# One network, two blocks: the first feed-forward unrolled, sums and prefetches spread, first tiles halved

## The reference, cut to what matters

```python
def conv_ffn(h, w_up, conv_w, conv_b, w_down, grid):
    gate, up = jnp.split(h @ w_up, 2, axis=-1)              # 1024 -> 2 x 2816
    gate = dwconv_grid(gate, conv_w, conv_b, grid)          # 3x3 depthwise; for the context a row of 256
    return (jax.nn.gelu(gate, approximate=True) * up) @ w_down

def swiglu(u, wg, wu, wd):
    return (jax.nn.silu(u @ wg) * (u @ wu)) @ wd

mod_l = jnp.split((jax.nn.silu(c) @ w_mod[layer] + b_mod[layer])[:, None, :], 6, axis=-1)   # latent
mod_c = jnp.split((jax.nn.silu(c_ctx) @ w_mod[layer] + b_mod[layer])[None, None, :], 6, axis=-1)
hl = modulate(rmsnorm(xl, norm_g[layer, 2]), mod_l[3], mod_l[4])     # h * (1 + scale) + shift
```

## Time and profile before

| | |
|---|---|
| median of 3 runs | 3651.16 us (3646.98 to 3659.4) |
| the profiled execution | 3651.36 us, its span 3649.6 us |
| mean granted clock of PE | 0.92 |
| PE busy | 3164.0 us (87%) |
| DVE busy | 2526.5 us (69%) |
| ACT busy | 1757.7 us (48%) |
| POOL busy | 389.5 us (11%) |
| transfers | 646.02 MB, mean 177 GB/s |

### The profile page before, as it was taken

One profiled execution on the slowest core, in us unless ns is written; L12 is line 12 of the kernel. 1 busy time (PEld: TensorE's weight loads), 2 busy tenths in 40 slices (PEclk: granted clock), 3 DMA queues, 4 the chain that ended last, 5 costly groups with the idle time before them and its releaser, 6 DMA issues. The chain is left out here.

```text
span 3649.6 us, 68684 instructions
## 1 busy us (share of the span) xinstructions
PE 3164.0 (87%) x27312; PEld 2626.4 (72%) x27312; DVE 2526.5 (69%) x3909; ACT 1757.7 (48%) x3042; POOL 389.5 (11%) x355
## 2 busy tenths in 40 slices
PE   5799876999969788877977799878799999999997
PEld 2654445887757477767976699654689889888986
DVE  1436665778874644576876678457599899989986
ACT  1223323112232575534441634336487788778775
POOL 0000002442100121106610011000000000000000
PEclk8899987999979999998978799877799999999998
DMA  8320011325632000036652398320399999999995
GB/s 336 82 83 1 1 46 52 92 92 173 248 98 63 3 5 5 4 123 217 210 194 65 120 365 308 122 72 8 105 371 350 355 362 369 351 356 361 371 347 196
DMA packets 270311, 646.02 MB, mean 177 GB/s; under 512 B 25277, under 2 KB 123689, under 8 KB 269929
## 3 DMA queue, kind: packets, MB, share of 16 engines
q1 hardware_dynamic: 248025, 562.62, 43.3%
q0 software_dynamic: 21312, 77.60, 5.9%
q10 hardware_dynamic: 720, 2.23, 0.2%
HBM read 641.34 MB, written 1.05 MB: 176 GB/s over the span
## 5 line engine op out<-in xcount | busy, mean ns | idle before, releaser
L3992 DVE TENSOR_TENSOR weights_lo<-raw_ring,weights_hi 128x896 fp32r<-128x896 f32 (+1 forms) x376 | 413.4, 1126 | 59.7 <-ACT weights_hi L3952 50.4
L344 PE MATMUL bank_pair<-x_hi,ring_hi 128*128 128x512 f32 (+1 forms) x928 | 349.2, 376 | 87.4 <-DVE x_lo L381 38.0
L3952 ACT ACTIVATE weights_hi<-raw_ring 128x896 fp32r<-128x896 f32 (+1 forms) x376 | 365.4, 981 | 98.0 <-PE bank_pair L3924 98.0
L344 PE MATMUL bank_pair<-x_hi,ring_lo 128*128 128x512 f32 (+1 forms) x928 | 343.7, 370 | 0.0
L3924 PE MATMUL bank_pair<-weights_hi,expert_x_hi 128*128 128x448 f32 x1024 | 296.8, 371 | 5.5 <-DVE weights_lo L3992 5.5
L3924 PE MATMUL bank_pair<-weights_hi,expert_x_lo 128*128 128x448 f32 x1024 | 291.5, 366 | 0.0
L3924 PE MATMUL bank_pair<-weights_lo,expert_x_hi 128*128 128x448 f32 x1024 | 291.5, 366 | 0.0
L3992 DVE TENSOR_TENSOR weights_lo<-H,weights_hi 128x896 fp32r<-128x896 f32 (+1 forms) x240 | 264.2, 1133 | 29.7 <-ACT weights_hi L3952 20.0
L3952 ACT ACTIVATE weights_hi<-H 128x896 fp32r<-128x896 f32 (+1 forms) x240 | 236.7, 989 | 72.7 <-PE bank_pair L3924 72.7
L344 PEld LDWEIGHTS bank_pair<-x_hi,ring_hi 128*128 128x128 f32 x928 | 180.4, 194 | 124.3 <-issue 59.2
L3924 PEld LDWEIGHTS bank_pair<-weights_hi,expert_x_hi 128*128 128x128 f32 x1024 | 190.6, 189 | 22.3 <-issue 5.3
(11 more groups left out here) (745 smaller groups left out, 7705.3 us busy)
## 6 DMA issues: line engine op xcount, KB each, us to landing
raw_ring<-in_moe_w_gate SPq DMA_DIRECT2D x72, 896.0 KB, 6.8
raw_ring<-in_moe_w_up SPq DMA_DIRECT2D x64, 896.0 KB, 7.1
ring_up<-in_ffn_w_up SPq DMA_DIRECT2D x110, 512.0 KB, 3.8
raw_ring<-in_moe_w_down SPq DMA_DIRECT2D x48, 1024.0 KB, 7.4
mod_ring_ada<-in_w_ada POOLq DMA_DIRECT2D x84, 512.0 KB, 6.4
H<-in_moe_w_up SPq DMA_DIRECT2D x48, 896.0 KB, 7.3
ring_down<-in_ffn_w_down SPq DMA_DIRECT2D x66, 512.0 KB, 6.9
H<-in_moe_w_down SPq DMA_DIRECT2D x32, 1024.0 KB, 7.4
```

What stands on the lines that cost most here:

```text
L344: ins = self.core.nc.tensor.matmul(self.banks[o][:, 0:moving.shape[1]], lhs, moving, start=(s == self.first[o] and k == 0 and i == 0), sto ...
L3952: nc.scalar.activation(hi[:, u % CUTS, 0:n].bitcast(F32R), raw_part(u), ACT.Copy).then_inc(cut.sem, 1)
L3992: nc.vector.tensor_tensor(lo[:, u % CUTS, 0:n].bitcast(F32R), raw_part(u)[:, 0:n], hi[:, u % CUTS, 0:n], ALU.subtract).then_inc(parted.sem, 1)
```

## The change

1. `ffn_stage` goes; `ffn_up_stage` serves both layers, unrolled, on `SplitGemm`. With 512 tokens it has three places for cut tiles, ten taps, and the gelu in ACT's order three tiles after the cut that frees the first bank (`gelu_after`), with 256 tokens four (it was two further on). x is cut into parts of Y and H.
2. In both, and in swiglu, the remainders of the first two tiles are DVE's (`rest_by`), tile 0 is cut and made in two halves, one for each output; a tile is cut before the x chunks that go with it, and PE waits for x chunk by chunk. `row_stage` does the first row in two halves.
3. The decoder's sums go in pairs (4, 5), (0, 2), (1, 3). 16 items, those of (4, 5), move into the first up stage, loaded by SP; 32 items (48 operations) stay in the down stage, and DVE's rate there is 2.5 operations a row instead of 2.2 items. Each block of sums is a tensor of its own. The latent stage's sums are loaded behind an iteration's tiles.
4. The prefetches of down weights go out one an iteration: from iteration 3 in the feed-forwards, from tile 8 at every fourth in swiglu.

```diff
@@ ModSums
-        self.items = [(j, k) for a in range(0, n_j, 2) for k in range(DC) for j in (a, a + 1)]
+        self.items = [(j, k) for pair in order for k in range(DC) for j in pair]
+    def ops_of(self, item):
+        return sum(i == item for i, _ in self.ops)
@@ SplitGemm
+    def pieces(self, n):
+        return (slice(0, P), slice(P, 2 * P)) if n == 0 else (slice(0, 2 * P),)
...
+        for cols in self.pieces(n):
+            self.core.nc.scalar.activation(self.hi[n % self.parts][:, 0:kc, cols].bitcast(F32R), self.ring[:, n % self.slots, 0:kc, cols], ACT.Copy).then_inc(self.cut.sem, 1)
...
         for j, o in enumerate(outs):
+            if n == 0 or j == 0:
+                self.wait_rested(pe, n, j if n == 0 else -1)
...
             for k in range(kc):
+                if it == 0 and j == 0:
+                    x.wait(pe, k0 + k)
@@ RowGemm
+    def load_ahead(self, sp):
+        if self.begun < min(self.slots, self.chunks):
+            self.load(sp, self.begun)
+            self.begun += 1
@@ row_stage
+        halves = lambda k: (slice(0, 2), slice(2, 4)) if k == 0 else (slice(0, 4),)
...
-                while waiting and len(sums) - len(waiting) < int((k + 1) * per_row):
+                while waiting and done + waiting[0].ops_of(waiting[0].taken) <= (k + 1) * ops_per_row:
+                    done += waiting[0].ops_of(waiting[0].taken)
                     waiting.pop(0).add(dve)
@@ FfnWeights
-            self.up = column_pairs(core, self.up_ctx, "up", [(up, 0), (up, FF)], FC // 2, ("pool",))
+        self.up = column_pairs(core, self.up_ctx, "up", [(up, 0), (up, FF)], FC // 2, ("dve", "dve", "pool"))
@@ ffn_up_stage
+        own = lambda i: tuple(core.sb(f"up_{n}{i}", [P, 4, 256], ctx=ctx)[:] for n in ("hi", "lo"))
+        g.open([p.const, own(0), own(1)] if T == TT else [p.X_ctx, p.H_ctx, p.Y_ctx, p.const])
+        x = XParts(core, DC, lambda k: st.H[:, k, here], p.Y[:, :, here], lambda k: p.H[:, k, here])
+        gelu_after = 3 if T == TT else 4
...
             for it in range(n_it):
                 for n in range(it * per, (it + 1) * per):
                     g.load_more(sp, n)
+                for _ in range(n_sums * it // n_it, n_sums * (it + 1) // n_it):
+                    sums.load(sp, "sp")
+                if it >= 3:
+                    weights.down.load_ahead(sp)
...
+                g.cut_tile(act, n)
                 for k in range(s * 4, s * 4 + 4) if it == 0 and s < 2 else ():
                     x.cut_chunk(act, k)
+                for due in range(n_it - 1):
+                    if n == due * per + g.parts + 1:
+                        middle_tap(due)
+                    if n == due * per + g.parts + gelu_after:
+                        gelu(due)
...
+            for n in (0, 1):
+                g.rest_of_tile(dve, nc.vector, n)
+                for k in range(4 * n, 4 * n + 4):
+                    x.rest_of_chunk(dve, k)
+            for it in range(n_it):
+                taps(it)
+                for _ in range(n_sums * it // n_it, n_sums * (it + 1) // n_it):
+                    sums.add(dve)
+                products(it)
@@ swiglu_stage
-                        if n == 2 * g.per:
-                            down.start(sp)
+                        if n % g.per == 0 and n >= 2 * g.per:
+                            down.load_ahead(sp)
@@ decoder_sums, build
+    return ModSums(core, st, f"mod{layer}", st.A["w_mod"][layer], ("b_mod", layer * 48), ((0, 48), (1, 16)), ((4, 5), (0, 2), (1, 3)))
+            ffn_up_stage(core, st, weights, 0, TT, sums, 16)
+            sums.sums_in(scope, (0, 1, 2, 3))
             ffn_down_stage(core, st, weights, sums)
```

More of the change, by code:

```diff
@@ L559, with __init__ @@
     WIDE = 1024
-    def __init__(self, core, st, scope, key, w, bias, vecs, slots=4, place=None):
+    def __init__(self, core, st, key, w, bias, vecs, order, slots=4):
         self.core, self.st, self.key, self.slots = core, st, key, slots
@@ L768, in _ @@
                     b = m.blocks.index((v, 2 * q + j // 2))
-                    ins = nc.tensor.matmul(core.bank(i % 4)[32 * j:32 * j + 32], st.C("ones")[:, 0:32], m.sums[:, b, j % 2 * 512:(j % 2 + 1) * 512], start=True, stop=True)
+                    ins = nc.tensor.matmul(core.bank(i % 4)[32 * j:32 * j + 32], st.C("ones")[:, 0:32], m.sums[b][:, j % 2 * 512:(j % 2 + 1) * 512], start=True, stop=True)
                 ins.then_inc(summed.sem, 1)
@@ L1078, in __init__ @@
         self.per = len(tiles)
-        self.rest_by = [rest_by[n % len(rest_by)] for n in range(len(self.tiles))]
+        self.rest_by = [rest_by[min(n, len(rest_by) - 1)] for n in range(len(self.tiles))]
+        assert self.rest_by[0] == "dve"
         self.kc = max(t[2] for t in tiles)
@@ L1167, in settle @@
             c.n += 16 * len(range(i, len(self.tiles), self.slots))
-        for c in (self.cut, self.consumed):
-            c.n += len(self.tiles)
+        self.cut.n += len(self.tiles) + 1
+        self.consumed.n += len(self.tiles)
         for c in self.freed.values():
@@ L1226, in start @@
     def start(self, sp):
-        self.begun = min(self.slots, self.chunks)
-        for k in range(self.begun):
-            self.load(sp, k)
+        while self.begun < min(self.slots, self.chunks):
+            self.load_ahead(sp)
+    def load_ahead(self, sp):
+        if self.begun < min(self.slots, self.chunks):
+            self.load(sp, self.begun)
+            self.begun += 1
     def raw(self, k):
@@ L1291, in _ @@
                     act.wait_ge(consumed.sem, consumed.at(k - S + 1))
-                nc.scalar.activation(places[k % S][0].bitcast(F32R), g.raw(k), ACT.Copy).then_inc(cut.sem, 1)
+                for q in halves(k):
+                    nc.scalar.activation(places[k % S][0][:, q].bitcast(F32R), g.raw(k)[:, q], ACT.Copy).then_inc(cut.sem, 1)
             for c in range(DC):
@@ L2173, in _ @@
             for it in range(n_it):
-                if it < n_sums:
-                    sums.load(sp, "sp")
                 for n in range(it * per, (it + 1) * per):
                     g.load_more(sp, n)
-                if it == 2:
-                    weights.down.start(sp)
-            for _ in range(n_it, n_sums):
-                sums.load(sp, "sp")
+                for _ in range(n_sums * it // n_it, n_sums * (it + 1) // n_it):
+                    sums.load(sp, "sp")
+                if it >= 3:
+                    weights.down.load_ahead(sp)
         @block.tensor
@@ L2189, in _ @@
         def _(pool):
-            for n in range(len(g.tiles)):
+            for n in range(2, len(g.tiles)):
                 g.rest_of_tile(pool, nc.gpsimd, n)
@@ L2239, in _, with products @@
                             g.bank_taken(ins, o)
-                for _ in range(n_sums * it // n_it, n_sums * (it + 1) // n_it):
-                    sums.add(dve)
+            def products(it):
                 for o in (0, 1):
```

221 lines of the change are left out of this document (68 added, 153 removed).

## The result

The changed kernel takes 3624.4 us (median of 4 runs, 3617.8 to 3630.0), 0.9919 of the kernel before, with a 95% interval of 0.9895 to 0.9943. Two later sets of runs gave 0.9924 (0.9906 to 0.9941) and 0.9915 (0.9902 to 0.9929). The forecast was 3628, from 3616 to 3643, and faster. The profiled execution took 3617.8 us, its span 3616.0.

What follows compares the result with a forecast made beforehand. PE, busy 87% of the span, was taken to bound the kernel, so only stage ends and other waits could move. Terms 3.0 - 0.7 + 6.1 + 7.3 + 5.0 + 2.3 + 0.2 = 23.2 us gave 3628, range 3616 to 3643.

Steps and rivals of the forecast that it cites:

- First up, start: First feed-forward's up projection: halves, DVE's remainders and chunk order let PE start earlier; gain 3.0 us, or 2.4.
- First up, middle: Same up projection: ACT's added cuts and the sums stay hidden, PE's pace unchanged; cost 0, bounds -4 to +6 us.
- The nearest row: Profile window of a stage keeping x where the new one will: 0.236 us per 512 columns, 2.7% slower, +6 us.
- First up, end: Same up projection: two adds stand before the last products; cost 0.7 us, 0 to 1.5.
- First down: First down projection: fewer adds per row save 5.2 us, an earlier start 0.9; together 6.1, between 3 and 7.
- Latent up: Latent up projection: DVE makes tiles 0 and 1, PE starts earlier without a second pause; gain 7.3 us, 4 if POOL is late.
- Swiglu: Swiglu: spreading six down transfers and an earlier start remove PE's starvation; gain 5.0 us, between 0 and 7.5.
- rival B: Swiglu stays starved if queues share 375 GB/s evenly, and POOL is late in the latent stage; 3636 us, chance 0.16.
- Row stages: Two attention output projections start earlier, 2.3 us; three other row stages give their start back, 0.2 in all.
- rival C: Earlier starts are given back because the next remainder, transfer or add takes the place; 3640 us, chance 0.16.

Runs made afterwards that it cites:

- x_first: Changed kernel, but in the three column stages x chunks 0 to 3 go ahead of tile 0 and 4 to 7 ahead of tile 1; 0.9950 of the kernel before.
- whole: Changed kernel, but every first tile and first row is cut and made whole, without halves; 0.9927 of the kernel before.
- pool_first: Changed kernel, but POOL makes the remainders of tiles 0 and 1 in both feed-forward up stages; 0.9931 of the kernel before.
- sums_back: Changed kernel, but all 48 items of the decoder's sums back in the first down projection, old pairs and rate; 0.9962 of the kernel before.
- burst: Changed kernel, but SP issues swiglu's six down transfers at once after tile 8; 0.9951 of the kernel before.
- y_weights: Changed kernel, but in the first up stage x's leading parts get their own tensor and two weight tiles' parts take Y's place; 0.9930 of the kernel before.

## Why the prediction was right

Its mechanism held, and its number, 3628, is 0.1% from the measured 3624. The gain is less close: 23.2 us were forecast, and 30.9 lie between the medians (3655.3 and 3624.4). The number came nearer than the gain because it was counted from 3651.2, the median of the first three runs of before, 4.1 us under that of the result. That part is luck. The terms, one by one:

- **First up, start, 3.0:** measured 2.8. At the first matmul the order brings 1.1 of it (x_first), the halves 0.36 (whole) and DVE for POOL nothing (pool_first), which pays behind it, where PE would pause 0.9. No run separates the rest, some 1.3. The working credited the halves with more than they bring.
- **First up, middle, 0:** the term that was mis-sized. PE's pace cost 2.1 us, inside the bounds of -4 to +6; the point where it would have been wrong, 172 matmuls in 40 us, was missed by one. The nearest row had the right sign, and x in Y's place was what it shared. By its own numbers, 0.236 against 40/175 = 0.2286 us, that row is 3.3% slower and not 2.7%, and the bound would have been +8; measured were 0.8%.
- **First up, end, 0.7:** 0. The adds end as PE ends.
- **First down, 6.1:** measured 8.3, with about 1 from the clock. The mechanism is shown by sums_back. The 5.2 us of listed waits were too few: in sums_back too the list falls 1.8 us short of the windows. Counting matmuls per window (37, 30 and 41 where 44 or 45 fit) gives what a list of waits misses.
- **Latent up, 7.3:** measured 7.1 between the means. DVE's first two tiles bring 4.7 of it (pool_first); without halves, or with x first, nothing is lost. The part for an early first half and first chunk was not what paid.
- **Swiglu, 5.0:** 6.2 to 6.7 by burst, 3.1 in the profile with a pause of 3.0 us; the range, 0 to 7.5, was the right thing to say. Even sharing between the queues would have left the sum near 0 (rival B); it wasn't near 0 in any profile.
- **Row stages, 2.5:** the attention outputs brought 1.3 for the first and some 1.9 for the second (28.3 and 28.4 us in its own length before, 25.9, 27.5 and 25.9 after). The start alone is 1.0 in each (PE's first matmul 1.81 us after the first cut instead of 2.77), so 1.9 of the 2.3 forecast for the two. What the second brings above that goes with the clock: it takes 25.9 us where the granted clock doesn't fall in it and 27.5 where it does, with the same code (the windows below, of the first and the second profile of after). The recurrent output, which I took as given back (0), lost 1.8: with halves its early start meets a second transfer wait of 2.3 us, and without them (whole) that wait is gone. That is rival C's mechanism in one stage, and worse than C had it. The latent down and swiglu down stages, where PE starts 1.0 earlier too, are 0.3 us shorter in sum: given back, as forecast.

```profile
2517.76:2543.76 26.00, 22.88 (x192) 22.70 (x192) 15.61 (x25) 13.97 (x25) 0.00 (x0) 1.00 0.25 82
2518.39:2544.39 26.00, 24.19 (x192) 24.22 (x192) 14.98 (x23) 12.40 (x22) 0.00 (x0) 0.93 0.25 82
```

The measured terms sum to 0.7 + 8.3 + 7.1 + 5.8 + 1.3 + 1.9 - 1.8 = 23.3 us, against 23.2 forecast. The three ratios stand for 28 to 31 us. The 4 to 8 us between aren't explained: untouched stretches differ by up to 17 us between profiles of kernels with the same code there, and also the medians of x_first and y_weights lie 12 and 6 us above after in the same rounds, where the stages they change account for 2 us and for none. The mean granted clock of the runs moves along with it: 0.9185 for before and 0.9212 for after in the rounds of the second set, 0.9181 and 0.9215 in those of the third, and there 0.9195 for y_weights and 0.9173 for x_first. So part of the gain may be a clock that falls less often, and the forecast had no term for that outside the stages touched; no run separates it from the change.

## What to carry to other kernels

When two engines share a first tile, and one of them slows the other down, give it all to one of them (here DVE) until PE has stock; only then bring in the second. An accumulation that waits for its own transfer must not stand ahead of a remainder that PE waits for: start it a row or two late, and size its share so that the engine stays under PE's pace. Split a first tile or row where nothing else is queued behind it, not where the next step waits for a transfer. Spread prefetches one by one into a queue that is already full, and expect a short pause in some executions even so.

## What was not expected of the hardware

- The same 128x512 matmuls at full clock ran at 175 or 173 in 40 us by where x's leading parts lay in SBUF, with no wait in either.
- Eight x remainders of 128x256 on DVE took 10.70 us while POOL made four tile remainders back to back, and 2.86 with POOL idle (twice 1.43).
- The same 192 matmuls of the second attention output took 25.9 or 27.5 us of stage, at a granted clock of 1.00 or 0.93 over its 26 us, in two executions of one kernel.
- An untouched stretch of some 610 us took between 609.2 and 626.8 us in 14 profiles, with 609 and 617 from one and the same kernel.
